# Mixture-of-experts layers in a two-block transformer kernel: quarter-width expert matmuls, neighbouring-row weight layout, and projection weights loaded one stage earlier

## The chip, the cores and the metric

The kernel runs on one core of one Trainium2 chip. The metric is the device time of one execution in microseconds (us). Three runs of the kernel before took 3566.93, 3572.45 and 3578.07 us; the median is 3572.45 us.

## The reference, cut to what matters

The program is two transformer blocks on 512 tokens of width 1024, all in float32. The first block has two layers; each ends in a mixture of experts, and these two mixtures are what the change rewrites. Per layer there are 16 experts, and each token goes to two of them:

```
def expert_block(args):
    xb, e = args
    hb = jax.nn.silu(xb @ w_gate[e]) * (xb @ w_up[e])
    return hb @ w_down[e]
...
x = layer_norm(ALPHA * x + moe(x, router_w, router_b, exp_w_gate[i], exp_w_up[i], exp_w_down[i]),
               ln_g[i, 1], ln_b[i, 1])
```

`w_gate[e]` and `w_up[e]` are 1024x512, `w_down[e]` is 512x1024, so one expert has three matrices of 2 MB. After the first layer's mixture comes an mLSTM mixer, whose input projection reads `ml_w_in`; after the second layer's mixture comes the second block, whose input projection reads `w_in_2` (the latent columns first). The second block ends in another expert stage of its own (16 experts of width 2048, called `ec` below), which the change leaves alone.

## The kernel before, in words

Each mixture is three stages, made by `moe_layer`. Between stages all engines meet at a barrier.

**route** (L1081). VectorE picks two experts per token and gives each token two rows in blocks of 96 rows, one expert to a block. SyncE meanwhile loads the three matrices of the first block. ScalarE has no work here.

**moe_experts** (L1247). The blocks are worked in pairs, r = 0 and r = 1, in a loop; in the profiled run a layer has 16 blocks in 8 pairs. Weights have two sets of buffers, one for each r. `moe_load` (L1242) brings one matrix with one DMA: row k*128+p of the matrix goes to partition p, so a partition gets 8 separate runs of 512 values (2 KB each) of gate and of up, and 4 runs of 1024 values (4 KB) of down. For one block TensorE does:

- `turn_x` (L1332): 8 transposes, in two halves of 4, bring the block's 96 rows of x into columns; ScalarE copies each half to `xg`. The second half uses the same PSUM bank as the first.
- `gate_up` (L1341): rows 0 to 63; 64 columns of the array do gate and the other 64 do up, 16 matmuls with 512 columns of the moving operand. A float32 matmul shows as two instructions, so 32 in the trace.
- `gate_up_tail` (L1352): rows 64 to 95; four strips of 32 columns of the array, each with a quarter of gate and up together, 32 matmuls (64 instructions) with 256 columns.
- ScalarE makes the sigmoid and copies the up half to SBUF, VectorE multiplies twice, for main and tail apart.
- `turn_h` (L1362): 6 matmuls with the identity bring the hidden rows into columns in the bank `h_ps`; VectorE copies them to `hT` (L1438, L1439).
- `down` (L1377): 64 rows in two halves of the array (16 instructions at L1385), then 32 rows in four strips (32 instructions at L1390). ScalarE empties the two banks (`rows_out`, L1481, L1482), GpSimd stores them to HBM (L1517, L1519).

The order on TensorE is written out by hand in `body`:

```
gate_up(i, 0)
turn_x(2 * i + 1, 1, i, 0)
gate_up_tail(i, 0)
turn_x(2 * i + 1, 1, i, 1)
gate_up(i, 1)
gate_up_tail(i, 1)
turn_h(i, 0)
...
```

and goes on with turn_x, down(i, 0), turn_x, turn_h(i, 1), down(i, 1). SyncE's queue (`load_pair`) reloads a buffer when it is free: gate and up of block r after its tail, down of both blocks after their `down`. The first block's x comes from 64 one-hot matmuls (`first_x`); GpSimd scatters all of x to HBM with 8 indirect DMAs, and later blocks' rows are read back from there (L1287).

**expert_sum** (L900). Two gathers per token tile, the weighted sum, the layer norm, and x transposed into `xT` for the next stage. SyncE is done after a few small loads.

Then `mlstm_inputs` (L1653) starts its own loads (L1694 to L1706): the gate columns `wg`, the first 384-column chunk, two copies of the gate bias, the convolution weights, the second chunk. Its first matmuls (L1739) wait for `wg` and both copies of the bias. In the second block, `gemms` (L157), called for "proj2", queues eight small side loads and then the first two weight chunks (L152); its first matmuls (L245) wait for chunk 0.

## Time and profile before

| what | value |
|---|---|
| median of three runs | 3572.45 us (3566.93 to 3578.07) |
| the profiled execution | 3572.37 us, its span 3570.0 us |
| TensorE (PE) busy | 3086.9 us, 86% |
| VectorE (DVE) busy | 1253.6 us, 35% |
| ScalarE (ACT) busy | 620.4 us, 17% |
| GpSimd (POOL) busy | 341.8 us, 10% |
| DMA | 886.20 MB, mean 248 GB/s |
| first block's mixtures | from 377 to 780 us and from 1150 to 1570 us of the span |
| the `ec` stage | about 2600 us to the end, 422 GB/s throughout |

A row of the timeline gives start, duration, engine, line, what is written from what, the count of instructions merged, and in brackets the idle time of the engine before it with what ended it. A matmul's duration is modelled and overlaps the next one's, so the distance between the starts of two groups is the time that the first one takes.

### The profile page before, as it was taken

The numbers are of one execution on the slowest core, as the hardware profiler recorded it, in microseconds if no ns is written. First come the engines' busy times: TensorE is split into PE (matmuls) and PEld (weight loads), VectorE is DVE, ScalarE is ACT, GpSimd is POOL, SyncE is SP. The second block draws the span as 40 slices with busy tenths as digits, with TensorE's granted clock in tenths as the row PEclk, the third lists the DMA queues.
The fourth block names the chain that finished last, engine by engine and source line by source line (L and its number), as shares of the span: only waits on it lengthen the run. The fifth ranks groups of instructions, "written<-read, shape, count | busy, mean of one in ns | idle before, by whom it ended". The sixth has DMA issues, their size and how long they took to land. (4 is left out here: it accounts for less than half of the span.)

```text
span 3570.0 us, 45399 instructions
## 1 busy us (share of the span) xinstructions
PE 3086.9 (86%) x17819; PEld 1460.8 (41%) x17819; DVE 1253.6 (35%) x2822; ACT 620.4 (17%) x1334; POOL 341.8 (10%) x434
## 2 busy tenths in 40 slices
PE   8889699949968799839999999889879888888887
PEld 5455444424444444324444444476433222332232
DVE  6533211133262111134999951175332111211122
ACT  1143122131321122130010021154100000000001
POOL 0023011110201111101000000014100000000000
PEclk9989799969988899959999999999889999999999
DMA  7861799922011999635333543591679999999997
GB/s 264 228 252 66 255 362 359 328 93 67 12 48 43 347 355 357 224 112 189 106 106 121 135 171 106 204 355 43 235 289 422 422 422 422 422 422 422 422 422 299
DMA packets 282432, 886.20 MB, mean 248 GB/s; under 512 B 35704, under 2 KB 75520, under 8 KB 233168
## 3 DMA queue, kind: packets, MB, share of 16 engines
q1 hardware_dynamic: 254032, 806.79, 60.3%
q0 software_dynamic: 28288, 77.91, 6.2%
q8 instruction: 71, 1.16, 0.1%
q14 instruction: 41, 0.34, 0.0%
HBM read 803.59 MB, written 80.99 MB: 248 GB/s over the span
## 5 line engine op out<-in xcount | busy, mean ns | idle before, releaser
L3060 PE MATMUL ec_gu<-ec_ring,ec_xg 128*32 128x512 f32 x4096 | 472.6, 605 | 98.3 <-DMA ec_ring<-in_w_up 97.4
L245 PE MATMUL proj_ps<-xT,proj_w 128*128 128x512 f32 x992 | 431.2, 597 | 0.0
L245 PE MATMUL proj_ps<-proj_w,xT 128*128 128x512 f32 (+2 forms) x896 | 360.7, 565 | 21.7 <-DMA proj_w<-in_w_in 21.7
L3060 PEld LDWEIGHTS ec_gu<-ec_ring,ec_xg 128*32 128x32 f32 x4096 | 123.6, 111 | 439.6 <-issue 295.3
L245 PEld LDWEIGHTS proj_ps<-xT,proj_w 128*128 128x128 f32 x992 | 189.5, 192 | 237.8 <-issue 237.6
L245 PEld LDWEIGHTS proj_ps<-proj_w,xT 128*128 128x128 f32 x896 | 172.4, 193 | 208.2 <-issue 156.3
L1349 PE MATMUL moe_gu_ps<-moe_w,moe_xg 128*64 128x512 f32 x1024 | 226.8, 595 | 18.4 <-ACT moe_xg L1464 16.8
L3096 PE MATMUL ec_yp<-ec_ring,ec_hT 128*64 128x512 f32 x1024 | 225.7, 595 | 7.0 <-issue 5.3
L274 ACT ACTIVATE proj_o<-proj_ps 128x512 f32<-128x512 f32 (+1 forms) x120 | 70.8, 590 | 611.4 <-PE proj_ps L245 611.3
L2239 DVE SCALAR_TENSOR_TENSOR band_big<-proj_hit,proj_row,band_big 128x516 f32<-128x516 f32 x256 | 173.5, 750 | 2.4
L2239 DVE SCALAR_TENSOR_TENSOR band_acc<-proj_hit,proj_row,band_acc 128x512 f32<-128x512 f32 x256 | 172.5, 746 | 2.4
L3153 DVE TENSOR_TENSOR xT<-xT,ec_gu 128x512 f32<-128x512 f32 x32 | 22.0, 688 | 374.6 <-ACT xT L3222 374.6
L1428 DVE TENSOR_TENSOR moe_sig<-moe_sig,moe_gu_ps 64x512 f32<-64x512 f32 x32 | 21.8, 680 | 374.2 <-ACT moe_up L1470 374.2
L3222 ACT ACTIVATE xT<-ec_gu 128x512 f32<-128x512 f32 x32 | 19.1, 598 | 771.1 <-PE ec_gu L3060 771.1
L1385 PE MATMUL moe_y_ps<-moe_w,moe_hT 128*64 128x512 f32 x512 | 125.4, 635 | 19.7 <-DVEq L1441 19.7
L3096 PEld LDWEIGHTS ec_yp<-ec_ring,ec_hT 128*64 128x64 f32 x1024 | 77.7, 137 | 142.8 <-issue 137.4
L1349 PEld LDWEIGHTS moe_gu_ps<-moe_w,moe_xg 128*64 128x64 f32 x1024 | 72.0, 137 | 154.0 <-issue 154.0
L1359 PE MATMUL moe_tgu_ps<-moe_w,moe_xg 128*32 128x256 f32 x2048 | 120.3, 388 | 0.0
L718 PE MATMUL mix_o<-out_w,xT 128*128 128x512 f32 x256 | 111.0, 593 | 2.6 <-PEq L89 2.6
L3183 DVE TENSOR_TENSOR ec_y<-ec_yp,ec_gate 64x512 f32<-64x512 f32 x32 | 22.0, 689 | 226.8 <-PE ec_yp L3096 226.6
L1748 PE MATMUL ml_ps<-xT,ml_w 128*128 128x512 f32 x224 | 96.4, 593 | 0.0
L1359 PEld LDWEIGHTS moe_tgu_ps<-moe_w,moe_xg 128*32 128x32 f32 x2048 | 64.2, 112 | 55.8 <-issue 16.9
(519 smaller groups left out, 3567.4 us busy)
## 6 DMA issues: line engine op xcount, KB each, us to landing
ec_ring<-in_w_gate SPq DMA_DIRECT2D x128, 1024.0 KB, 24.5
ec_ring<-in_w_up SPq DMA_DIRECT2D x128, 1024.0 KB, 27.0
ec_ring<-in_w_down SPq DMA_DIRECT2D x128, 1024.0 KB, 26.0
moe_w<-in_exp_w_gate SPq DMA_DIRECT2D x32, 2048.0 KB
moe_w<-in_exp_w_up SPq DMA_DIRECT2D x32, 2048.0 KB
moe_w<-in_exp_w_down SPq DMA_DIRECT2D x32, 2048.0 KB, 18.8
proj_w<-in_w_in SPq DMA_DIRECT2D x22, 2048.0 KB, 11.0
proj_w<-in_w_ada SPq DMA_DIRECT2D x16, 1536.0 KB
```

The costliest lines, as they stand in the source:

```text
L245: mm = nc.tensor.matmul(bank[0:jb["op"], 0:jb["ow"]], lhs, rhs, start=(k == 0), stop=(k == nk - 1))
L274: e = nc.scalar.activation(row, bank, jb["func"], scale=jb["scale"])
L718: mm = nc.tensor.matmul(o_ps[t % 2][q][:], xT[:, k, t * P:(t + 1) * P], w[q][:, k, :], start=(k == 0), stop=(k == KD - 1))
L1349: mm = nc.tensor.matmul(gu_ps[r][part, :], xg[r][:, k, 0:MAIN], w[r][n][:, k * D_EXP:(k + 1) * D_EXP], start=(k == 0), stop=(k == KD - 1))
L1359: mm = nc.tensor.matmul(tgu_ps[r][q * TAIL:(q + 1) * TAIL, :], xg[r][:, k, MAIN:MB], w[r][n][:, c0:c0 + 256], start=(k == 0), stop=(k == K ...
L1385: nc.tensor.matmul(y_ps[part, :], hT[r][:, f, 0:MAIN], w[r][2][:, c0:c0 + 512], start=(f == 0), stop=(f == KF - 1))
L1748: mm = nc.tensor.matmul(bank[:], w[m % 2][:, kk, g * P:(g + 1) * P], xT[:, kk, :], start=(kk == 0), stop=(kk == KD - 1))
L2239: V.scalar_tensor_tensor(acc[:, h, 0:wd], self.hit[r][:, 0:wd], self.row[r][:, h:h + 1], acc[:, h, 0:wd], ALU.mult, ALU.add)
L3060: mm = nc.tensor.matmul(gu_ps[2 * g + m][q * TG:(q + 1) * TG, :], xg[:, k, c0:c0 + TG], cols[:, :, q, :], start=(k == 0), stop=(k == KD - 1))
L3096: mm = nc.tensor.matmul(y_ps[half, :], hT[:, f * CAP:(f + 1) * CAP], w[:, j * D + hh * 512:j * D + (hh + 1) * 512], start=(f == 0), stop=( ...
L3153: V.tensor_mul(hid[g], sig[g], gu_ps[2 * g][:])
L3183: e = V.tensor_mul(y[lo if ex == 0 else hi, n_of(hh)], y_ps[half, :], gt2[half, n_of(hh)])
```

## The change

- The expert matrices are laid out with neighbouring rows in a partition: row 8p+k of gate and up, row 4p+k of down. A partition's share of a matrix is one run of 16 KB in HBM. Gate and up of one r lie in one buffer `gu`.
- x must match: in route, ScalarE copies each token tile of x (128x1024) into the space of `xT` so that columns p*8+k become k*128+p; `first_x` and the scatter read this copy.
- Gate and up of all 96 rows are computed as three groups of 32 rows in four strips of the array, 96 matmuls with 256 columns per block; the moving operand is 128 columns of gate and 128 of up. The hidden rows come out as 32-row strips, so VectorE's 32x32 transpose makes `hT` directly. `turn_h`, the ScalarE copies of up, `h_ps` and the two VectorE copies go.
- The order on TensorE becomes gate_up(0), gate_up(1), turn_x, down(0), turn_x, down(1); `turn_x` has two banks. The first pair is written out ahead of the loop with turn_x(1) between its gate_ups.
- ml_w_in's gate columns and first two chunks, and proj2's first two chunks, are loaded by SyncE during expert_sum, after its gathers have landed. Each set of buffers is freed later with one more barrier.

```
@@ expert_sum, SyncE
+                if ahead:
+                    for t in range(NT):
+                        sp.wait_ge(got[t], 32)
+                    ahead(sp)
@@ route
+            @block.scalar
+            def _(act):
+                xp = rows_by_partition(xT)
+                for t in range(NT):
+                    nc.scalar.activation(xp[:, t, :].rearrange("a (k p) -> a k p", p=P),
+                                         x[:, t, :].rearrange("a (p k) -> a k p", p=P), ACT.Copy)
@@ moe_load
-    sp.dma_start(w[n][:], weights[n][ds(e, 1)].rearrange("a (k p) n -> p (a k) n", p=P)).then_inc(w_ready[n], 16)
+    sp.dma_start(w[n], weights[n][ds(e, 1)].rearrange("a (p k) n -> p (a k) n", p=P)).then_inc(w_ready[n], 16)
@@ moe_experts
+        cols_of = lambda r, k, q: gu[r][:].rearrange("p (m k q c) -> p m k q c", m=2, k=KD, q=Q)[:, :, k, q, :]
@@ SyncE, load_pair
                     for r in range(2):
-                        sp.wait_ge(turned, 4 * i + 2 * r + 3)
+                        sp.wait_ge(turned, 4 * i + 2 * r + 2)
                         rows(2 * i + 2 + r, r)
-                        sp.wait_ge(tail_ready, 2 * i + r + 3)
+                    for r in range(2):
+                        sp.wait_ge(gu_ready, 4 * i + 2 * r + 2)
                         moe_load(sp, w[r], w_ready[r], weights, 0, e[r])
                         moe_load(sp, w[r], w_ready[r], weights, 1, e[r])
@@ TensorE
+                    pe.wait_ge(gu_taken, 2 * b + 1)
+                    for g in range(GROUPS):
+                        for k in range(KD):
+                            for q in range(Q):
+                                mm = nc.tensor.matmul(gu_ps[r][q * TAIL:(q + 1) * TAIL, g * 256:(g + 1) * 256],
+                                                      xg[r][:, k, g * TAIL:(g + 1) * TAIL], cols_of(r, k, q),
+                                                      start=(k == 0), stop=(k == KD - 1))
+                        if g >= 1:
+                            mm.then_inc(gu_ready, 1)
...
+                def downs(i, more):
+                    for r in range(2):
+                        if more:
+                            turn_x(2 * i + 2 + r, r, i + 1 + r)
+                        down(i, r)
                 def body(i, more):
                     gate_up(i, 0)
                     gate_up(i, 1)
+                    downs(i, more)
...
+                gate_up(0, 0)
+                turn_x(1, 1, 1)
+                gate_up(0, 1)
+                downs(0, True)
+                with pe.Fori(1, n1) as i:
                     body(i, True)
@@ VectorE, for the pieces (groups 0 and 1, group 2)
+                        V.tensor_mul(sig[r][:, g, :], sig[r][:, g, :], gu_of(r)[:, g, 0, :])
+                        V.drain()
+                        V.tensor_mul(hid[r][:, g, :], sig[r][:, g, :], gu_of(r)[:, g, 1, :]).then_inc(gu_taken, 1)
+                        V.drain()
+                        e = V.transpose(hT[r][:].rearrange("p f (g t) -> p g f t", t=TAIL)[:, g, :, :],
+                                        hid[r][:, g, :].rearrange("p g (t f) -> p g f t", t=TAIL))
@@ mlstm_inputs
-                pe.wait_ge(g_in, 48)
+                pe.wait_ge(wg_in, 16)
@@ class MixerWeights
+    def fetch(self, sp):
+        sp.dma_start(self.wg[:], self.cols[:, :, 2 * ML_W:2 * ML_W + 16]).then_inc(self.wg_in, 16)
+        self.load(sp, 0)
+        self.load(sp, 1)
@@ second_block
-                gemms(nc, "proj2", jobs, ahead=(begin[id(gate_job)] - 1, bb.first),
+                gemms(nc, "proj2", jobs, ahead=(begin[id(gate_job)] - 1, bb.first), held=ws[0], begun=2,
...
+            nc.clear_and_free_semaphores(ws[0].ready)
+            nc.all_engine_barrier()
```

In `mlstm_inputs` the gate bias now has a semaphore of its own, on which VectorE waits before it uses the bias. `wg`, the chunk buffers and their semaphores move to `MixerWeights`.

## Rows read from the trace of the kernel before

**Rows 1.** The page's costliest groups: gate and up of rows 0 to 63.

```profile
L1349 PE MATMUL moe_gu_ps<-moe_w,moe_xg 128*64 128x512 f32 x1024 | 226.8, 595 | 18.4 <-ACT moe_xg L1464 16.8
```

**Rows 2.** Busy time by stretches: two pairs; then PEclk, DMA share, GB/s.

```profile
534.09:573.46 39.37, 37.19 (x332) 16.71 (x328) 5.54 (x12) 8.88 (x17) 6.09 (x12) 1.00 1.04 357
653.91:694.99 41.08, 38.91 (x333) 17.12 (x329) 5.54 (x12) 8.88 (x17) 6.09 (x12) 0.96 1.04 357
```

**Rows 3.** Timeline of TensorE in the pair that starts at 534.09.

```profile
534.09 7.09 PE L1349 MATMUL moe_gu_ps<-moe_w,moe_xg 128*64 128x512 f32 x32
541.10 0.55 PE L1337 MATMUL moe_x_ps<-ident,moe_xs 96*128 96x96 f32 x4
541.58 3.66 PE L1359 MATMUL moe_tgu_ps<-moe_w,moe_xg 128*32 128x256 f32 x64
545.17 0.55 PE L1337 MATMUL moe_x_ps<-ident,moe_xs 96*128 96x96 f32 x4
...
559.79 3.65 PE L1385 MATMUL moe_y_ps<-moe_w,moe_hT 128*64 128x512 f32 x16 [0.43 <-DVEq L1441]
563.38 1.93 PE L1390 MATMUL moe_ty_ps<-moe_w,moe_hT 128*32 128x256 f32 x32
565.24 0.55 PE L1337 MATMUL moe_x_ps<-ident,moe_xs 96*128 96x96 f32 x4
```

**Rows 4.** DMA totals of two stretches: 534.1:573.5, and 2700:3400.

```profile
DMA packets 5842, 14.05 MB, mean 357 GB/s; under 512 B 325, under 2 KB 325, under 8 KB 5842
...
DMA packets 40555, 295.34 MB, mean 422 GB/s; under 512 B 4505, under 2 KB 4505, under 8 KB 4505
```

**Rows 5.** Timeline of that pair: GpSimd stores what ScalarE has emptied.

```profile
567.01 1.12 POOL L1517 DMA_DIRECT2D slots<-moe_y  x2 [27.38 <-ACTq L1483]
```

**Rows 6.** Timeline of TensorE: starts of pairs, last down of layer 0.

```profile
407.78 7.09 PE L1349 MATMUL moe_gu_ps<-moe_w,moe_xg 128*64 128x512 f32 x32 [0.88 <-ACT moe_xg L1464]
...
455.33 7.09 PE L1349 MATMUL moe_gu_ps<-moe_w,moe_xg 128*64 128x512 f32 x32
...
694.99 7.09 PE L1349 MATMUL moe_gu_ps<-moe_w,moe_xg 128*64 128x512 f32 x32
...
732.02 1.93 PE L1390 MATMUL moe_ty_ps<-moe_w,moe_hT 128*32 128x256 f32 x32
1181.60 7.09 PE L1349 MATMUL moe_gu_ps<-moe_w,moe_xg 128*64 128x512 f32 x32 [0.86 <-ACT moe_xg L1464]
...
1228.48 7.09 PE L1349 MATMUL moe_gu_ps<-moe_w,moe_xg 128*64 128x512 f32 x32
...
1469.84 7.09 PE L1349 MATMUL moe_gu_ps<-moe_w,moe_xg 128*64 128x512 f32 x32
```

**Rows 7.** Timeline of the first pair in layer 0, then layer 1.

```profile
420.46 0.90 PE L1337 MATMUL moe_x_ps<-ident,moe_xs 96*128 96x96 f32 x4 [5.60 <-DMA moe_xs<-slots]
421.29 5.82 PE L1359 MATMUL moe_tgu_ps<-moe_w,moe_xg 128*32 128x256 f32 x64
...
1190.86 0.38 SPq L1244 DMA_DIRECT2D moe_w<-in_exp_w_up  x1
...
1201.74 4.51 PE L1349 MATMUL moe_gu_ps<-moe_w,moe_xg 128*64 128x512 f32 x20 [1.60 <-DMA moe_w<-in_exp_w_up]
```

**Rows 8.** Timeline of route in layer 0: VectorE's last instruction.

```profile
395.36 0.15 DVE L1239 TENSOR_SCALAR blk_e<-route_nbl 128x1 int32<-128x1 f32 x1
```

**Rows 9.** Timeline: end of expert_sum, start of mlstm_inputs; proj2's start.

```profile
773.55 5.73 ACT L1049 ACTIVATE xT<-exp_t,exp_ccol 128x128 f32<-128x128 f32 x16
...
780.07 0.41 SPq L1694 DMA_DIRECT2D ml_wg<-in_ml_w_in  x1
...
788.14 8.41 PE L1739 MATMUL ml_ps<-xT,ml_wg 128*4 128x512 f32 x64 [12.43 <-DMA ml_gb<-in_ml_gate_bT]
...
1570.83 0.33 SPq L2148 DMA_DIRECT2D proj_pki<-in_pos_k  x1
...
1584.19 36.09 PE L245 MATMUL proj_ps<-proj_w,xT 128*128 128x352 f32 x112 [17.71 <-DMA proj_w<-in_w_in]
```

More of the change, by code:

```diff
@@ L897, in _, with expert_sum @@
                         e.then_inc(y_pool[i], 1)
-def expert_sum(nc, name, x, xT, ident, sbr, y, gain, shift, second=None, h=None):
+def expert_sum(nc, name, x, xT, ident, sbr, y, gain, shift, second=None, h=None, ahead=None):
     posA, posB, wA, wB, _ = sbr
@@ L1483, in rows_out, with rest @@
                     nc.scalar.drain().then_inc(y_copied, 1)
-                def body(i, more):
-                    main(i, 0)
-                    copy_x(2 * i + 1, 1, 0)
-                    tail(i, 0)
-                    copy_x(2 * i + 1, 1, 1)
-                    main(i, 1)
-                    tail(i, 1)
-                    if more:
-                        copy_x(2 * i + 2, 0, 0)
-                    rows_out(i, 0)
-                    if more:
-                        copy_x(2 * i + 2, 0, 1)
-                    rows_out(i, 1)
-                copy_x(0, 0, 0)
-                copy_x(0, 0, 1, h_ps)
-                with act.Fori(0, n1) as i:
+                def rest(i, more):
+                    for r in range(2):
+                        if more:
+                            copy_x(2 * i + 2 + r, r)
+                        rows_out(i, r)
+                def body(i, more):
+                    gates(i, 0)
+                    gates(i, 1)
+                    rest(i, more)
+                copy_x(0, 0)
+                gates(0, 0)
+                copy_x(1, 1)
+                gates(0, 1)
+                rest(0, True)
+                with act.Fori(1, n1) as i:
                     body(i, True)
@@ L3249, in second_block, with latent_weights, fetch @@
     with nc.sbuf_tensor("h", [P, NT, D], F32) as h, ExitStack() as held:
+        n_lat = Q_RANK + KV_RANK + ROPE
+        hf = h[:].rearrange("p t d -> p (t d)")
+        rows = hf[:, 0:NT * n_lat].rearrange("p (t f) -> p t f", t=NT)
+        lat_job = job(win, 0, 2, n_lat // 2, xT, P, S, None, "N",
+                      sb=lambda j, g: rows[:, g, j * (n_lat // 2):(j + 1) * (n_lat // 2)])
+        first = ExitStack()
+        ws = []
+        def latent_weights():
+            ws.append(WeightSlots(nc, first, "proj2", 2, KD * 512, False, side="right"))
+            def fetch(sp):
+                for j in range(2):
+                    ws[0].load(sp, lat_job, j, j)
+            return fetch
         moe_layer(nc, 1, a, x, xT, cst, slots, y_dram, sbr, escore,
-                  [ln(a["ln_g"][1, 1], a["ln_b"][1, 1]), rms(a["g_norm_mix_2"][0], sh1, sc1)], h=h)
-        n_lat = Q_RANK + KV_RANK + ROPE
+                  [ln(a["ln_g"][1, 1], a["ln_b"][1, 1]), rms(a["g_norm_mix_2"][0], sh1, sc1)], h=h, ahead=latent_weights)
         gates = dram("gates", [S, 2 * D])
```

221 lines of the change are left out of this document (85 added, 136 removed).

## The prediction

> **What bounds the kernel now.** I first read the page's table of busy shares: TensorE is busy 86% of the span, so a change pays where it shortens TensorE's own sequence or a wait in it. The page's costliest groups then say who is waited for in the mixtures: the idle time ahead of gate and up was ended by ScalarE's copy of x, 16.8 of 18.4 us, and not by the weight loads [rows 1]. So the mixture loop runs at TensorE's pace.
>
> The busy times by stretches show how near the next limit is. In one pair of blocks, 39.37 us, TensorE is busy 37.19 us, and the DMA engines have a share of 1.04 at 357 GB/s [rows 2]: they are full too. The DMA totals say with what: 5842 packets for 14.05 MB, every one under 8 KB. From 2700 to 3400 us, in the `ec` stage, 36,050 of 40,555 packets are 8 KB or more and the same engines move 422 GB/s [rows 4]. Two things hold the pair near 39.4 us, and a change of one alone gives little.
>
> The timeline of TensorE prices the parts of a pair by the distance between starts [rows 3]: 64 instructions of the tail 545.17 - 541.58 = 3.59 us, half a turn of x 541.58 - 541.10 = 0.48 us, the two parts of down 3.59 and 1.86 us, together 5.45 us. A second kind of pair takes 41.08 us instead of 39.37, at a mean granted clock of 0.96 instead of 1.00 [rows 2]: in it a short stretch runs at 1.2 GHz, for 1.7 us more. Three of the layer's pairs 1 to 6 in layer 1 and two in layer 0 are of that kind.
>
> **The change, part by part.**
>
> *A steady pair.* Gate and up of a block become 192 instructions of the tail's form, 128 rows by 32 columns of the array with 256 moving columns: 3 x 3.59 = 10.77 us, 21.54 us for two. Column work is what it was (the old parts take 7.01 + 3.59 = 10.60 us), only the moving operand lies in two runs. No row here has two runs in just this way; the cost of that is between nothing (the `ec` stage feeds four runs of 128 columns) and a few per cent, and I take nothing. Four half turns are 1.92 us, two downs 10.90 us. Sum 34.36 us. `turn_h` and the waits for VectorE's copies of it go, and so does ScalarE's copy of x between two gate_ups, since a block's x is now turned a whole down ahead. VectorE gets a 32x32 transpose instead, beside TensorE's other work: gate_up(1) and a turn cover block 0's chain, turn and down(0) cover block 1's.
>
> What is late next: down(1) waits until ScalarE has emptied the banks of down(0), and only one turn of x, 0.96 us, is left in between where turn_h stood. GpSimd, which waits for the same signal, starts at 567.01, 1.77 us after down(0) ends at 565.24 [rows 3, 5]. The bounds are 0 and 1.77 - 0.96 = 0.8 us; GpSimd's own start is in that, so I take 0.5 us. A steady pair: 34.9 us.
>
> *Can DMA keep up?* A pair needs 12.58 MB of weights and 1.57 MB of x and y rows. One run of 16 KB per partition makes a packet at least as long as the `ec` stage's. At 422 GB/s the weights take 29.8 us; the small rows at today's 357 take 4.4 us; 34.2 us, just under 34.9. Buffers give room besides: gate and up of block 0 are issued at 10.8 us of a pair and needed at 34.9, and take 10 us. So TensorE still sets the pace. The upper bound is today's 357 GB/s, 39.6 us a pair (a rival below). DMA is the next bound, at once.
>
> *Pairs 1 to 6.* Layer 0: 694.99 - 455.33 = 239.7 us now, 6 x 34.9 = 209.4 after, 30.3 less. Layer 1: 1469.84 - 1228.48 = 241.4, 32.0 less [rows 6]. That counts the slow-clock stretches as gone, since TensorE's gaps shrink to one of 0.5 us a pair; if they stay in every pair it is 12 x 1.7 = 20 us worse.
>
> *The last pair.* Now 694.99 to 732.02 + 1.93, 39.0 us. After: 21.54 + 5.45 + 5.45 us and, with no turn between the downs, a wait of about 1.5 us: 33.9. 5.1 us less in each layer, 10.2 us.
>
> *The first pair* takes 47.55 us in layer 0 and 46.88 in layer 1 [rows 6]. gate_up(0, 0) is 10.8 us. The x rows of block 1 come only after the scatter, at 420.46, 12.7 us after the pair's start, so TensorE waits about 2 us instead of 5.6 [rows 7]. Then gate_up(0, 1) stands ahead of what used to fill the time, and waits for up of block 1. In layer 1 that load is issued 9.3 us into the pair (1190.86 - 1181.60) and ended a wait 10.9 us later, at 20.1 [rows 6, 7]. With longer packets it lands between 5.0 us after the x rows (2.1 MB at 422), at 17.7, and those 20.1; I take 18.7, nearer the first, since the stage with long packets is the nearest row for them. Behind such a wait the clock is at 1.2 GHz for a while: the tail at 421.29 took 5.8 us where 3.6 is usual [rows 3, 7], 2.2 us more. 18.7 + 10.8 + 2.2 + 13.3 (turns, downs, 0.5 wait) = 45.0 us. 2.5 and 1.9 us less.
>
> *Route.* ScalarE gets four copies of 128x1024 with a stride of 8 elements in the read. By its row with 16 pieces of 128 columns in 5.73 us [rows 9], 1024 columns take at most 2.9 us if the stride is free, four 11.5 us, and the stride may add to that. They stand beside VectorE's chain, which ends at 395.36, 18 us after the stage begins [rows 8]. I take nothing; without that cover it would be the 11.5 us and more. The gathers' and scatters' sizes don't change.
>
> *Early loads.* In mlstm_inputs the first matmul started at 788.14, 8.1 us after the stage's first instruction, held by the last small load [rows 9]. After, `wg` and chunk 0 have landed; VectorE still waits for the bias, but needs it only when the gate matmuls (8.4 us) are done. TensorE starts at about 780.4: 7.7 us less. In proj2 the first matmul goes from 1584.19 to about 1571.1: 13.1 us less. VectorE and ScalarE work there on what TensorE delivers, so they move with it and I count the gain as kept. The loads themselves, 3 MB at most, run in expert_sum behind its gathers, where no other large transfer is. SyncE waits there for the gathers, and nothing is queued behind it. Two added barriers: from ScalarE's last end, 773.55 + 5.73 = 779.28, to the next stage's first instruction, 780.07, is 0.8 us [rows 9]; 1.6 us more.
>
> *Sum:* 30.3 + 32.0 + 10.2 + 2.5 + 1.9 + 7.7 + 13.1 - 1.6 = 96.1 us less. Against the profiled execution's 3572.4 us that is 3476.3. The median shown, 3572.45, is the same to 0.1 us. About 0.3% (11 us) is what a measurement of this kernel can tell from no change.
>
> **The rivals.**
>
> *Slow clock stays or comes.* Every steady pair has a stretch at 1.2 GHz, 1.7 us each. For it: the rows have it in five of twelve pairs, always in the later down. Against: the gaps ahead of it shrink. 3476 + 20 = 3496. Chance 0.10.
>
> *The early loads buy nothing*, because another engine or load sets those stages. Against: TensorE waits for exactly these transfers [rows 9]. 3476 + 21 = 3497. Chance 0.06.
>
> *DMA becomes the bound* at today's 357 GB/s, because the loads' rate is not set by the packets, or because they stay cut at 2 KB. Then a pair takes 14.15 MB / 357 = 39.6 us. The buffers' room, some 7 us at the first steady pair, is eaten at 4.7 us a pair, so some 4.5 of six pairs pay 4.7 us: 21 us a layer, 42 in all, 3518. Against it: 422 GB/s with 8 KB packets on the same engines [rows 4], and there each load of 1 MB to 128 partitions already travels as runs of 8 KB. The Trainium skill's page "DMA: Bandwidth & Descriptors" (Specifications) speaks for this rival: it says that transfers of 512 B and up reach line rate, and gives about 358 GB/s as a core's share of HBM, so 16 KB runs would bring nothing over 2 KB. By that rule the time would be 3518. The trace has exactly such a figure, 357, in the mixtures, but the 422 of the `ec` stage goes against both halves of it. Chance 0.11.
>
> *Slower than before.* A single run of 16 KB into one partition might be worse than short ones: only 8 such packets an engine per matrix, and the stores of y take turns with them. It decides where DMA time per pair passes today's 40 us by more than the rest gains, at some 14.15 MB / 42 us = 337 GB/s. At 300 GB/s a pair takes 47.2 us, 7 us more than now in 12 pairs, 84 us, less about 20 us of early loads: 3572 + 64 = 3636. No row has packets over 8 KB in numbers; up to 8 KB longer was faster. Chance 0.04. A change that comes to nothing by several of these together has 0.02.
>
> **How the numbers follow.** The forecast has a chance of 0.67, so the predicted time is its 3476. Its own range comes from the bounds: 7 us less without the wait for emptied banks, 4 us less in the first pairs, 2 to 3 us in the early loads, so 3462; and 5 to 10 us more from two runs in the moving operand and half the slow stretches. With the first two rivals the range reaches to 3508, which leaves out DMA's two cases and the last, 0.17. Faster by over 0.3%: 0.94; within: 0.02; slower: 0.04.
>
> **What would show it.** Right: distances of 34.5 to 35.5 us between starts of pairs; DMA packets of 16 KB, some 128 per matrix, and over 400 GB/s while loads run; a DMA share clearly under 1.0 at times; idle time ahead of down(1) ended by ScalarE; first matmuls of mlstm_inputs and proj2 within 1 us of their stages' starts. Wrong: idle time ahead of gate_up ended by a weight load in steady pairs; gate_up over 11.2 us a block; ScalarE's four copies ending after VectorE's chain in route; the first pair over 48 us.

## The result, and the profile after

The changed kernel takes 3472.87 us (median of 4 runs), the kernel before 3574.84 on the same chip: ratio 0.971, 95% interval 0.9693 to 0.9728, 102 us less. The prediction was 3476.3. That the number fits hides two errors of 15 and 13 us that cancelled, and a third in what was credited to the early loads. The profiled execution of the changed kernel is the fastest of its four (3464.36 us; the others 3466.67, 3479.07 and 3480.73), so the profiles show a larger difference than the medians. First the page of the changed kernel: span, TensorE, the group that answers to [rows 1], all packets of the execution.

```profile
span 3462.0 us, 50697 instructions
PE 3025.1 (87%) x20507; PEld 1482.5 (43%) x20507; DVE 1244.6 (36%) x2822; ACT 576.8 (17%) x1266; POOL 341.6 (10%) x434
...
DMA packets 212814, 886.41 MB, mean 256 GB/s; under 512 B 35704, under 2 KB 75520, under 8 KB 151248
...
L1366 PE MATMUL moe_gu_ps<-moe_gu,moe_xg 128*32 128x256 f32 x6144 | 338.4, 382 | 8.7 <-DMA moe_gu<-in_exp_w_up 7.5
```

TensorE is busy 2% less. ScalarE's copy of x no longer ends the idle time ahead of gate and up. The packets went from 282432 to 212814, 69618 fewer: 64 gate and up matrices less 896 packets each and 32 down matrices less 384 each would be 69632, so the long runs are there.

A layer has eight pairs, counted 0 to 7: pair 0 is the first, pairs 1 to 6 are the steady ones, pair 7 is the last. The timeline of TensorE, an undisturbed pair (it answers to [rows 3]), and a later one:

```profile
483.90 20.90 PE L1366 MATMUL moe_gu_ps<-moe_gu,moe_xg 128*32 128x256 f32 x384
504.73 0.88 PE L1353 MATMUL moe_x_ps<-ident,moe_xs 96*128 96x96 f32 x8
505.55 3.65 PE L1380 MATMUL moe_y_ps<-moe_w,moe_hT 128*64 128x512 f32 x16
509.13 1.93 PE L1385 MATMUL moe_ty_ps<-moe_w,moe_hT 128*32 128x256 f32 x32
510.99 0.88 PE L1353 MATMUL moe_x_ps<-ident,moe_xs 96*128 96x96 f32 x8
512.23 3.65 PE L1380 MATMUL moe_y_ps<-moe_w,moe_hT 128*64 128x512 f32 x16 [0.36 <-ACTq L1460]
515.81 1.93 PE L1385 MATMUL moe_ty_ps<-moe_w,moe_hT 128*32 128x256 f32 x32
517.56 20.90 PE L1366 MATMUL moe_gu_ps<-moe_gu,moe_xg 128*32 128x256 f32 x384
...
608.63 0.88 PE L1353 MATMUL moe_x_ps<-ident,moe_xs 96*128 96x96 f32 x8 [2.08 <-DMA moe_xs<-slots]
609.44 5.35 PE L1380 MATMUL moe_y_ps<-moe_w,moe_hT 128*64 128x512 f32 x16
```

The undisturbed pair is 517.56 - 483.90 = 33.66 us. The later one waits 2.08 us for the x rows of the next pair, and behind that wait the same 16 instructions take 5.35 us instead of 3.65. Six pairs of the twelve steady ones have such waits: 0.70, 2.08 and 0.57 us in layer 0, 0.17, 1.71 and 2.84 in layer 1, and the three of 1.7 us and more are each followed by a slow down. Pairs 1 to 6 average 34.5 us in layer 0 and 35.0 in layer 1.

Both kinds of pair by stretches (clock, DMA share and GB/s at the end, as in [rows 2]), then the DMA view of 455:645, its rate in 40 slices and its totals:

```profile
483.90:517.56 33.66, 33.30 (x500) 18.07 (x496) 5.02 (x12) 4.82 (x12) 6.09 (x12) 1.00 1.01 406
...
585.65:623.15 37.50, 35.07 (x500) 18.48 (x496) 5.00 (x12) 4.81 (x12) 6.09 (x12) 0.95 1.01 401
```

```profile
GB/s 422 326 396 425 428 435 420 425 371 357 401 438 406 432 438 422 327 365 424 428 434 421 424 372 311 414 435 428 428 428 415 287 381 428 428 415 437 424 350 336
DMA packets 8507, 76.39 MB, mean 402 GB/s; under 512 B 1807, under 2 KB 1807, under 8 KB 4401
```

The engines are as full as before by their share, but move 402 GB/s instead of 357 [rows 2]. The rate is not even: about once a pair it falls to some 290 to 370. That dip turned out to be the story behind the waits: two blocks need 12.58 MB of weights and 1.57 MB of rows, and 14.15 MB at 402 GB/s take 35.2 us, more than the 33.66 us of TensorE. The undisturbed pair above moves 406 GB/s x 33.66 us = 13.67 MB, so the transfers fall behind by 0.5 MB in it; the buffers hide that for some pairs, then TensorE waits.

Where the 108.0 us of the two profiled executions went (spans 3570.0 and 3462.0), by distances between marks in the two timelines: expert stage of layer 0 from first gate and up to last down 326.2 to 284.3 (41.9 less), layer 1 327.2 to 286.6 (40.7), from the experts' end to the mixer's first matmul 54.2 to 45.9 (8.3), to the last projection's 75.4 to 61.4 (14.0), mixer to the next experts 393.5 to 388.3 (5.2), ahead of the first experts 1.6 less, behind the last projection's start 3.6 more. The forecast's 96.1 us had 76.9 in the experts (82.6 here) and 19.2 in the early loads with their barriers (22.3 here); the other 3.2 it did not have.

### The profile page after: what moved, and what is told of

It is laid out like the page before. It is cut to its first block and busy times, and to the rows that moved or that the text cites. A ratio compares the mean times of both kernels' runs of the same rounds, so it can differ in the third digit from the quotient of the medians.

```text
span 3462.0 us, 50697 instructions
## 1 busy us (share of the span) xinstructions
PE 3025.1 (87%) x20507; PEld 1482.5 (43%) x20507; DVE 1244.6 (36%) x2822; ACT 576.8 (17%) x1266; POOL 341.6 (10%) x434
## 2 busy tenths in 40 slices
DMA packets 212814, 886.41 MB, mean 256 GB/s; under 512 B 35704, under 2 KB 75520, under 8 KB 151248
## 5 line engine op out<-in xcount | busy, mean ns | idle before, releaser
L1366 PE MATMUL moe_gu_ps<-moe_gu,moe_xg 128*32 128x256 f32 x6144 | 338.4, 382 | 8.7 <-DMA moe_gu<-in_exp_w_up 7.5
L1366 PEld LDWEIGHTS moe_gu_ps<-moe_gu,moe_xg 128*32 128x32 f32 x6144 | 201.4, 111 | 142.0 <-issue 11.1
L1421 DVE TENSOR_TENSOR moe_sig<-moe_sig,moe_gu_ps 128x256 f32<-128x256 f32 x64 | 22.7, 355 | 482.8 <-ACT moe_sig L1452 482.8
L1752 PE MATMUL ml_ps<-xT,mlw 128*128 128x512 f32 x224 | 96.4, 593 | 0.0
L3035 PE MATMUL ec_x<-ec_sel,h 128*128 128x128 f32 x576 | 70.9, 283 | 11.1 <-ACT ec_xg L3219 6.2
L3035 PEld LDWEIGHTS ec_x<-ec_sel,h 128*128 128x128 f32 x576 | 67.5, 196 | 19.7 <-ACT ec_xg L3219 7.9
## 6 DMA issues: line engine op xcount, KB each, us to landing
moe_w<-in_exp_w_down SPq DMA_DIRECT2D x32, 2048.0 KB, 18.7
```

Of the source, the lines that this page charges most:

```text
L1366: mm = nc.tensor.matmul(gu_ps[r][q * TAIL:(q + 1) * TAIL, g * 256:(g + 1) * 256], xg[r][:, k, g * TAIL:(g + 1) * TAIL], cols_of(r, k, q), ...
L1752: mm = nc.tensor.matmul(bank[:], w[m % 2][:, kk, g * P:(g + 1) * P], xT[:, kk, :], start=(kk == 0), stop=(kk == KD - 1))
L3035: mm = nc.tensor.matmul(x_ps[:, c * P:(c + 1) * P], h[:, t, cc * P:(cc + 1) * P], sel[:, t, :], start=(t == 0), stop=(t == NT - 1))
```

## The experiments

Twelve kernels, numbered by subject, not in the order in which they ran. Times are medians, ratios are against runs of the kernel before on the same chip. The experiments ran on several chips, on which the kernel before has medians from 3572.66 to 3578.16 us, and each median stands for 4 to 10 runs: a difference of some 5 us between two of the kernels below is not told from none by their medians, and the traces have to tell it. The length of a pair is the distance between the starts of its gate and up and the next one's.

**1. Short runs again for gate and up.**

```
-                                         x[:, t, :].rearrange("a (p k) -> a k p", p=P), ACT.Copy)
+                                         x[:, t, :].rearrange("a (k p) -> a k p", p=P), ACT.Copy)
...
-    sp.dma_start(w[n], weights[n][ds(e, 1)].rearrange("a (p k) n -> p (a k) n", p=P)).then_inc(w_ready[n], 16)
+    rows = "a (k p) n -> p a k n" if n < 2 else "a (p k) n -> p a k n"
+    src = weights[n][ds(e, 1)].rearrange(rows.replace("p a k n", "p (a k) n"), p=P)
+    sp.dma_start(w[n], src).then_inc(w_ready[n], 16)
```

> The changed kernel with its gate and up matrices loaded as before the change (128 partitions times 8 runs of 2 KB per matrix, instead of 16 KB in one run), and x copied by ScalarE without the reordering; the down matrices keep the long runs, the narrow matmuls and the early loads stay. Theory A (the long runs are what lets the queue keep up with the faster loop): the two gate and up pairs of matrices, 8.39 MB, go at the old 357 GB/s, 23.5 us, the other 5.3 MB at the new 405, 13.0 us, so a pair takes about 36.5 us or more where the changed kernel's undisturbed pairs take 33.66 and its mean of pairs 1 to 6 is 34.5 and 35.0; the DMA's share stays at 1.00 and the rate falls from 402 towards 375 GB/s. Time 3473 + 12 x 1.5 to 12 x 2.9 = 3491 to 3508. Theory B (the length of a run doesn't matter here, TensorE alone sets the pair): pairs stay at 33.7 to 35, time 3473 within 5 us.

Measured: 3509.54 us, ratio 0.9816 (0.98 to 0.9832), 36.7 more than the changed kernel. Timeline of TensorE in pair 2 of layer 0, and the DMA view of 455:645:

```profile
508.54 1.52 PE L1355 MATMUL moe_x_ps<-ident,moe_xs 96*128 96x96 f32 x8 [2.54 <-DMA moe_xs<-slots]
509.99 4.64 PE L1382 MATMUL moe_y_ps<-moe_w,moe_hT 128*64 128x512 f32 x16
```

```profile
GB/s 423 428 250 310 388 388 397 405 428 436 236 322 387 387 402 406 428 432 234 335 387 386 402 406 444 411 234 348 387 389 398 414 432 407 225 365 386 391 398 420
DMA packets 25743, 71.50 MB, mean 376 GB/s; under 512 B 1628, under 2 KB 1628, under 8 KB 24436
```

Theory A holds: from pair 2 on every pair waits, 37.4 to 38.3 us in layer 0 and 37.8 to 40.7 in layer 1, at 376 GB/s. It came out 1.5 us above the upper end (3508). The expectation had divided 13.67 MB, what an undisturbed pair moves; a pair needs 14.15 MB, and at 376 GB/s these take 37.6 us, as in layer 0. Layer 1's pairs of 40.4 us are longer than that; in nine of the ten pairs that wait the first 16 matmuls of a down take 4.6 to 6.1 us instead of 3.65, and whether that is what lengthens them was not tested. The narrow matmuls need the long runs.

**2. Long runs alone, in the kernel before.** The load of gate and up takes `(p k)`, ScalarE's four copies are added in `route`, the experts read `rows_by_partition(xT)`; nothing else.

> The kernel before with one part of the change alone: gate and up matrices in 16 KB runs and x reordered by ScalarE into xT during the routing stage, which the expert stage reads as its rows; half-width matmuls, short runs of the down matrices and late loads stay. Theory A (the old loop was set by TensorE, 39.37 us a pair with its queue at the limit beside it): the pairs stay at 39.0 to 39.4, time 3570 to 3575. Theory B (the old loop was set by the queue): pairs fall to about 36.5 as two thirds of its bytes go faster, 14 x 2.5 = 35 us less, 3535 to 3545.

Measured: 3575.64 us, ratio 0.9999 (0.9989 to 1.0008). Two pair starts (the first gate and up of a pair has no wait):

```profile
495.97 7.09 PE L1362 MATMUL moe_gu_ps<-moe_w,moe_xg 128*64 128x512 f32 x32
508.61 7.09 PE L1362 MATMUL moe_gu_ps<-moe_w,moe_xg 128*64 128x512 f32 x32 [1.00 <-ACT moe_xg L1477]
535.35 7.09 PE L1362 MATMUL moe_gu_ps<-moe_w,moe_xg 128*64 128x512 f32 x32
```

39.38 us a pair, as before. So the long runs of gate and up alone are worth nothing: the old loop was set by TensorE. The pairs of 41.0 to 41.1 us are still there too, one in layer 0 and four in layer 1.

**3. Late loads.** Both early loads undone: `mw.fetch(sp)` is the first thing of the mixer's input stage, and the last projection has `begun=0`.

> The changed kernel with both early loads undone: the first weights of the mLSTM input stage are asked for when that stage begins, as before, and none of the weights of the last projection is asked for ahead of its stage; the expert stages are those of the change. Theory A (each stage began with a wait for its weights that the early load removes): first matmul of the mLSTM inputs 8 us later against the end of the experts (45.9 us there in the changed kernel, 54.2 in the one before), that of the last projection 14 us later (61.4 against 75.4): 3473 + 22 = 3495. Theory B (the loads only take up the queue earlier and what they gain is lost again in the summing stage): within 5 us of 3473.

Measured: 3492.10 us, ratio 0.9777 (0.9754 to 0.98), 19.2 more than the changed kernel, near theory A's 22. The profiled execution is the fastest of its four (3475.88; the others 3491 to 3505), so the marks in the trace carry more than the median. They divide it otherwise. Timeline of TensorE, first matmul of each of the two stages, here and in the changed kernel:

```profile
737.28 9.79 PE L1744 MATMUL ml_ps<-xT,mlw_g 128*4 128x512 f32 x64 [6.59 <-DMA mlw_g<-in_ml_w_in]
...
1485.99 34.37 PE L245 MATMUL proj_ps<-proj_w,xT 128*128 128x352 f32 x108 [17.88 <-DMA proj_w<-in_w_in]
```

```profile
736.39 8.72 PE L1743 MATMUL ml_ps<-xT,mlw_g 128*4 128x512 f32 x64 [4.40 <-PEq L89]
...
1472.62 40.31 PE L245 MATMUL proj_ps<-proj_w,xT 128*128 128x352 f32 x128 [4.40 <-PEq L89]
```

Against the experts' end the projection starts 13.6 us later (75.0 against 61.4), as expected. The mixer starts 2.4 us later (48.3 against 45.9) and not 8. The rest must come from something that this experiment left in: the gate bias.

**4. x rows ahead of the down matrices.**

```
 def load_pair(i):
-    for r in range(2):
-        sp.wait_ge(turned, 4 * i + 2 * r + 2)
-        rows(2 * i + 2 + r, r)
...
     for r in range(2):
+        sp.wait_ge(turned, 4 * i + 2 * r + 6)
+        rows(2 * i + 4 + r, r)
         sp.wait_ge(down_ready, 2 * i + r + 1)
         moe_load(sp, w[r], w_ready[r], weights, 2, e[r])
```

(With the first pair's rows asked for ahead of the loop, room for one more pair of rows, and TensorE's wait for them at the end.)

> The changed kernel with the rows of x of pair i+2 asked for as soon as those of pair i+1 have been transposed, so ahead of the down matrices in the queue instead of behind them (and one pair of rows too many at the end, that nobody reads). Theory A (the waits for x rows come of the order of the queue): the waits of 0.7, 2.1, 0.6 us in the first layer and 0.2, 1.7, 2.8 in the second go, 8.1 us, and with the three of 1.7 us or more the slow downs behind them (3 x 1.7 us): pairs 1 to 6 all at 33.7, time 3473 - 10 to 13 = 3460 to 3463. Theory B (the queue is full in this loop, share 1.01, so that something must be late): the same time is lost to waits for a gate, up or down matrix instead, the pairs still average 34.5 and 35.0, time 3470 to 3475.

Measured: 3477.20 us, ratio 0.9737 (0.972 to 0.9754). Waits of TensorE in layer 0 (us in total, times, longest), here and in the changed kernel:

```profile
PE moe_gu_ps L1368 <- DMA moe_gu<-in_exp_w_up: 20.2, 10, 4.1
PE moe_y_ps L1382 <- ACTq L1464: 3.7, 8, 1.2
```

```profile
PE moe_x_ps L1353 <- DMA moe_xs<-slots: 6.4, 4, 3.1
PE moe_y_ps L1380 <- ACTq L1460: 3.7, 8, 1.2
PE moe_gu_ps L1366 <- DMA moe_gu<-in_exp_w_up: 3.3, 1, 3.3
```

Theory B in its mechanism: no wait for x rows is left in the steady pairs, and nine more for a gate or up matrix took their place (ten against one); five of layer 0's six steady pairs take 34.4 to 38.2 us. It had 3470 to 3475 and the averages of before; layer 0 averages 36.6 us instead of 34.5, layer 1 34.4 instead of 35.0, and the median is 2.2 us above its range. Order in the queue was not what was short.

**5. Up of block 1 ahead of the wait for the scatter.** The second `moe_load` of block 1 moves above `sp.wait_ge(put, ...)`.

> The changed kernel with the up matrix of block 1 asked for before the queue waits for the scattered rows, not after it. Theory A (TensorE waits in the first pair for that matrix because SP sat in the wait): the 3.3 us and 4.2 us before gate and up of block 1 go, the first pair takes 40 instead of 44.0 and 43.3, time 3473 - 6 to 8 = 3465 to 3467. Theory B (the queue is full, the rows of block 1 are then later by the 5 us that 2 MB take): the wait moves to the transposition of block 1, which waits 3.1 and 3.0 us already, and the first pair stays within 1 us of 44.0 and 43.3: no change.

Measured: 3469.04 us, ratio 0.9711 (0.9693 to 0.9729). The first pair of layer 0 in the timeline, here and in the changed kernel:

```profile
423.57 1.54 PE L1353 MATMUL moe_x_ps<-ident,moe_xs 96*128 96x96 f32 x8 [5.90 <-DMA moe_xs<-slots]
425.69 12.61 PE L1366 MATMUL moe_gu_ps<-moe_gu,moe_xg 128*32 128x256 f32 x192 [0.58 <-ACT moe_xg L1445]
```

```profile
406.23 10.57 PE L1366 MATMUL moe_gu_ps<-moe_gu,moe_xg 128*32 128x256 f32 x192 [0.58 <-ACT moe_xg L1445]
419.89 1.54 PE L1353 MATMUL moe_x_ps<-ident,moe_xs 96*128 96x96 f32 x8 [3.09 <-DMA moe_xs<-slots]
424.74 12.74 PE L1366 MATMUL moe_gu_ps<-moe_gu,moe_xg 128*32 128x256 f32 x192 [3.31 <-DMA moe_gu<-in_exp_w_up]
```

Theory B: the wait for the matrix went (0.58 us is left), that for the rows grew from 3.09 to 5.90, and the first pairs are 43.96 and 43.15 us, where they were 44.01 and 43.28. In this trace layer 0's steady pairs have no wait at all (all 33.66 or 33.67 us) and three of layer 1's wait 0.92 to 3.14 us, with the edit outside the steady pairs: how many of them wait differs from one execution to the next.

**6. Both edits together.**

> Rows ahead and up first in one kernel. Theory A: the sum of the two, 3473 - 16 to 20 = 3453 to 3457. Theory B (the queue is full in the pairs, so moving loads in it can't shorten them): 3470 to 3475.

Measured: 3479.42 us, ratio 0.9739 (0.9714 to 0.9764). No gain, as theory B said, but 4.4 us above its range; in the trace layer 0's pairs 1 to 6 take 218.2 us and layer 1's 203.5, where the changed kernel has 207.2 and 210.2, and the waits are for gate and up matrices.

**7. Less traffic: no y stores in the loop.** GpSimd's `store` keeps its wait and its release of the buffer and loses the six transfers.

> The changed kernel without the y stores inside the loop (GpSimd only hands the buffers back; the last pair's stores stay), so the sums behind it read other rows: a part of the traffic is left out, nothing else. Theory A (the loop's transfers fill the 16 engines, and the waits for x rows are what does not fit): 0.79 of 13.67 MB a pair goes, the queue needs 12.88 / 0.406 = 31.7 us, the DMA's share falls to about 0.94, all pairs 1 to 6 take 33.66 and the slow downs behind the waits go: 3473 - 13 = 3460, and the first pair is shorter by up to 1 us. Theory B (the waits come of the place of the x rows in the queue, behind the down matrices, with room in the queue): waits of 0.6 to 2.8 us stay, 3473 within 5.

Measured: 3456.94 us, ratio 0.9679 (0.9658 to 0.9701), 15.9 less than the changed kernel. All twelve steady pairs take 33.66 to 33.71 us: theory A for the time. Not for the share. The DMA view of one pair, 484:517.6, slices of 0.84 us:

```profile
GB/s 488 390 390 488 429 449 410 390 488 361 327 244 224 361 176 244 283 307 380 468 390 390 488 371 429 468 429 449 410 390 488 371 410 468 449 449 390 410 488 371
DMA packets 1082, 13.27 MB, mean 395 GB/s; under 512 B 128, under 2 KB 128, under 8 KB 320
...
q1 hardware_dynamic: 1082, 13.27, 101.1%
```

SP's queue alone fills the engines, at a lower rate, where it had 94.5% beside the stores. So a share of 1.0 doesn't say that no more bytes would fit: there are nine slices in a row, 7.6 us, in which the engines are busy and move 176 to 361 GB/s. The record of single packets says the same: from 492 to 499.5 us a packet of 16 KB takes 0.89 us on average, where it takes 0.62 before and after. No store is in this kernel, so the dip isn't theirs. The two 384 KB loads of x rows, issued at 484.0, land 15.5 us later in the median, at about 499.5, as the dip ends. The dip is not gone here, and still no steady pair waits: the 13.37 MB that are left to a pair take 34.2 us at the 391 GB/s of 455:645, and the buffers cover six times 0.5 us.

**8. Short runs in all three matrices.** Experiment 1 with each down matrix in four transfers of 4 KB runs.

> The kernel of the first experiment (gate and up in 2 KB runs, 3509.5 us) with the down matrices too in four transfers of 4 KB runs each instead of one of 16 KB, so that every matrix has the runs of before and only the narrow matmuls, the layout in SBUF and the early loads are left of the change. Theory A (every byte then goes at the 357 GB/s of the old loop): 13.67 MB / 357 = 38.3 us a pair as the least, against the 37.5 and 39.5 that the first experiment's pairs average: pairs 38.3 to 41, time 3510 to 3530. Theory B (4 KB is long enough, 2 KB alone is short): the same as the first experiment within 5 us, 3505 to 3514.

Measured: 3513.99 us, ratio 0.9826 (0.9809 to 0.9843), 4.5 us over experiment 1, whose interval (0.98 to 0.9832) it overlaps. 364 GB/s in 455:645, against 376. Inside both theories' ranges, so not settled: 4 KB runs of the down matrices cost 4.5 us or nothing. It shows what the narrow matmuls are worth without any long run: the expert stages take 313.0 and 303.2 us here, against 326.2 and 327.2 in the kernel before and 284.3 and 286.6 in the changed one, so 37 of the 83 us gained there. Its pairs 1 to 6 average 39.2 us in layer 0, where 14.15 MB at 364 GB/s would take 38.9.

**9. 128 rows of x in a load instead of 96.**

```
-        xs = [st.sb(f"xs{r}", [MB, D]) for r in range(2)]
+        xs = [st.sb(f"xs{r}", [P, D]) for r in range(2)]
...
-                    sp.dma_start(xs[r][:], slots_dram[ds(b * MB, MB), :]).then_inc(xs_ready[r], 16)
+                    sp.dma_start(xs[r][:], slots_dram[ds(b * MB, P), :]).then_inc(xs_ready[r], 16)
```

(The transposes read `xs[r][0:MB, ...]`.)

> The changed kernel with 128 rows of x in each load of a block instead of 96 (the 32 more are the next block's and are not used): 0.26 MB more a pair. Theory A (96 rows use 96 of the 128 partitions and so only part of the paths into SBUF, which is why the rate falls to 176 to 361 GB/s while they land): the dip goes, 1.05 MB at 406 take 2.6 us where 0.79 MB at 270 take 2.9, pairs the same or shorter, 3465 to 3473. Theory B (the reads of the rows themselves are slow, whatever they are written to): 1.05 MB at 270 take 3.9 us, 1.0 more a pair, the waits for x rows grow by that in pairs 2 to 6 of each layer and bring more slow downs: 3480 to 3490.

Measured: 3451.00 us, ratio 0.9649 (0.9628 to 0.9671), 21.9 less than the changed kernel, and the fastest of all. The DMA view of 455:645 and a pair's row among the busy times by stretches:

```profile
GB/s 423 414 439 415 439 421 417 434 417 436 422 428 438 422 430 423 426 432 421 431 417 436 438 406 436 424 428 425 432 437 401 443 425 431 428 422 433 404 445 431
DMA packets 9150, 81.07 MB, mean 427 GB/s; under 512 B 1850, under 2 KB 1850, under 8 KB 4858
```

```profile
483.90:517.56 33.66, 33.30 (x500) 18.07 (x496) 5.01 (x12) 4.82 (x12) 6.08 (x13) 1.00 1.01 427
```

Theory A. More bytes go and the dip is gone: no slice is under 401 GB/s. All twelve steady pairs take 33.66 or 33.67 us and no down runs slow. The two profiled executions differ by 11.7 us (3450.3 and 3462.0), 3.5 of it in layer 0's experts and 8.3 in layer 1's; the medians differ by more. The changed kernel's four runs spread over 16 us and these over 7, and experiment 5 shows its waits differing between executions; that this makes up the rest is likely and not shown. The packets tell the same as the rate: from 495 to 503 us, while the 128 rows of two blocks land, one of 16 KB takes 0.61 us and one of the rows 0.16, where 96 rows took 0.26 each in experiment 7.

The Trainium skill bears on this: its page "SBUF — State Buffer" (Door 1: The DMA port swizzle) says that a transfer's bandwidth depends on how many of 16 ports its partitions reach, with partitions 0 to 63 on eight of them and 64 to 127 on the other eight. Rows 0 to 95 then load eight ports twice as much as the rest. This agrees in direction. By that rule alone 96 rows take as long as 128, so padding would cost nothing but gain nothing either; the measured gain is larger than that, and which engine writes which row no run here shows.

**10. x rows through GpSimd's queue.** GpSimd asks for block b + 4 right before it stores block b.

> The changed kernel with the x rows of blocks 1 and later asked for by GpSimd in its own queue, right after the down matmuls that free the buffer's y, instead of by SP behind the down matrices. Theory A (in the loop the 16 engines have only just enough time, whatever the queue, as the fourth and the seventh experiment say): x rows never wait, but a gate or up matrix does, as in the fourth experiment: pairs 1 to 6 average 34.5 to 36, time 3470 to 3480. Theory B (what costs the time is that the x rows go in one lump through one queue: in the DMA view of the seventh experiment's pair the rate is 390 to 488 GB/s except for 6.7 us at 176 to 361 in the stretch where they land; beside the weights of the other queue they are spread out): no wait for rows nor for matrices, pairs 1 to 6 all at 33.7, 3473 - 13 = 3460, and no slice of a pair under 350 GB/s.

Measured: 3501.29 us, ratio 0.9795 (0.9775 to 0.9814), 28.4 more than the changed kernel; neither theory had that. Timelines of GpSimd and of TensorE in layer 0:

```profile
472.48 0.52 POOL L1482 DMA_DIRECT2D moe_xs<-slots  x1 [16.43 <-issue]
473.12 1.13 POOL L1501 DMA_DIRECT2D slots<-moe_y  x2
```

```profile
523.48 1.54 PE L1349 MATMUL moe_x_ps<-ident,moe_xs 96*128 96x96 f32 x8 [5.99 <-DMA moe_xs<-slots]
```

The first pairs wait 10.6 and 9.8 us for rows (49.1 and 47.6 us instead of 44.0 and 43.3), every second pair after them 2.7 to 6.5 us, and slices of 275 to 331 GB/s remain in the DMA view of 480:530. GpSimd waits for its stores to land before it goes on, and 384 KB of rows now stand in the same queue ahead of them; that this is what delays it is my reading. As a test of spreading the rows it is spoilt by that, and settles nothing.

**11. The bias's wait alone, in the kernel before.** `pe.wait_ge(g_in, 48)` becomes 16, and the two bias loads count on a semaphore that VectorE waits for.

> The kernel before with one wait moved: in the mLSTM input stage TensorE waits for its gate weights alone, and the gate bias has a semaphore of its own that VectorE waits for, as in the changed kernel; all loads stay where they were. Theory A (the start at 788.14 was held by the bias, a transfer of 0.1 KB that stands behind 1.5 MB of the first weight chunk in the queue, and the early load itself is worth only the 2.4 us that the third experiment showed): first matmul 2.2 us after the first issue at about 780.1, so near 782.5, 5.7 us earlier, the chunk behind it then waits for its own 1.5 MB until some 786 or not at all as the gate matmuls take 8.4 us; time 3575 - 5 = 3570. Theory B (the weights set the start): 788.1 as before, no change.

Measured: 3573.92 us, ratio 0.9994 (0.9985 to 1.0004): as a time not to be told from no change, nor from the 4.6 us below, as the interval goes from 5 us less to 1 us more. The profiled execution is the second slowest of ten (3581.74 us): all its twelve steady pairs take 41.07 us, where the kernel before has five such in its profile, on the same code. The timeline shows the start:

```profile
790.15 8.68 PE L1740 MATMUL ml_ps<-xT,ml_wg 128*4 128x512 f32 x64 [7.85 <-DMA ml_wg<-in_ml_w_in]
```

The idle time ahead of that matmul is 12.43 us in the kernel before [rows 9], 7.85 here, 6.59 with late loads, 4.40 in the changed kernel. So 4.6 us of the 8.0 belong to the bias, which no longer holds TensorE from behind the first 1.5 MB of weights, and 2.2 to the early load; 1.3 lie in other differences between this kernel and that of experiment 3.

**12. Short runs of gate and up with 128 rows.**

> The first experiment's kernel (gate and up in 2 KB runs, 3509.5 us, 36.7 more than the changed kernel) with 128 rows of x in each load of a block, as in the ninth, which took the changed kernel to 3451 us with all its pairs at 33.66 and a rate of 427 GB/s without a dip. Theory A (2 KB runs are slower in themselves: in the DMA view of the first experiment the gate and up matrices go at 382 to 410 GB/s outside the dip): 8.39 MB / 390 = 21.5 us and the other 5.96 MB at 427 = 14.0, 35.5 us a pair as the least against 33.66 that TensorE needs; 3451 + 12 x 1.8 = 3473 at least, with slow downs 3473 to 3490. Theory B (the dips of the 96 rows were all that made the short runs matter): pairs at 33.7, 3451 to 3458.

Measured: 3477.88 us, ratio 0.9725 (0.9708 to 0.9741). From pair 4 on, 35.65 to 35.70 us in both layers, against theory A's 35.5; TensorE's wait in such a pair:

```profile
601.27 3.01 PE L1368 MATMUL moe_gu_ps<-moe_gu,moe_xg 128*32 128x256 f32 x52 [1.34 <-DMA moe_gu<-in_exp_w_up]
```

Theory A: 404 GB/s in 455:645 against 427, and 14.42 MB at 404 GB/s take 35.7 us, which is what the pairs take. Single packets show why: outside any dip one of 2 KB takes 84 to 88 ns, one of 4 KB 159, one of 8 KB 313 (`ec` stage of the kernel before, 2700 to 3400 us), one of 16 KB 612, so 23 to 24 bytes per ns for the shortest and 26.8 for the longest. So the 36.7 us of experiment 1 are not the price of short runs alone: with 128 rows they cost 26.9 us (3477.88 - 3451.00), and what is late is a gate or up matrix instead of the rows.

## Why the prediction was right, and where it was not

*A steady pair*: predicted 34.9 us, measured 33.66. The two gate_ups take 504.73 - 483.90 = 20.83 us, 54.2 ns an instruction, where 56.1 came from the old tail's 64 instructions; that row held the start of a phase in every 64, and six phases in a row have fewer seams, which is my reading, not a test. Turns 0.82 and 0.88 us instead of 1.92 together; downs 5.44 and 5.33 where 5.45 was taken; the wait for emptied banks 0.36 us where 0.5 was taken, 1.16 in the last pair where 1.5 was.

*Can DMA keep up?* This is the step that failed. It said 34.2 us of transfers in 34.9 us, so "TensorE still sets the pace", with the weights at 422 GB/s and the rows at 357, 414 together. The 14.15 MB were right, but the rate is 402, so 35.2 us: while 96 rows land, everything on the engines falls to 176 to 361 GB/s (experiment 7). That is more than the 33.66 us of TensorE and more than the forecast's 34.9; the buffers cover it for some pairs, and six of twelve wait, 8.1 us and 5.0 us of slow downs, 13 in all. By luck twelve pairs at 1.24 us under the forecast are worth 15. Experiment 9 shows the cause: without the dip the engines move 427 GB/s, which is what 14.42 MB in 33.66 us ask for, and no steady pair waits. Behind the wrong rate stands a wrong reading of [rows 4]. I took all of the difference between 357 and 422 GB/s for the price of short packets. But a loop that TensorE paces moves 14.15 MB in 39.37 us whatever the engines could do, which is 359 GB/s, so the 357 was no measure of their limit (the new loop with the same runs, which does wait for its transfers, gets 364, experiment 8); and the kernel before has the dip as well, as its rate in 455:645 shows:

```profile
GB/s 409 412 343 293 387 311 313 392 408 412 401 248 377 361 257 379 405 410 415 286 331 389 269 340 397 409 415 308 304 374 295 317 370 381 394 420 269 338 381 257
```

With 2 KB runs of gate and up the new loop moves 376 GB/s with the dip and 404 without (experiments 1 and 12), with 16 KB runs 402 and 427: the dip costs 25 to 28 GB/s, the short runs of gate and up 23 to 26. My sign for room, a DMA share clearly under 1.0, never came, not even with fewer bytes; it is no measure of room.

*Pairs 1 to 6* together: 207.2 and 210.2 us, predicted 209.4, by the luck above. *Last pair*: 33.0, predicted 33.9. *First pair*: 44.0 and 43.3, predicted 45.0; gate_up(0, 1) starts 18.5 and 18.7 us into it, predicted 18.7. That the late issue of up of block 1 makes that wait is right only in part: asked for earlier (experiment 5), the matrix swaps places with the rows and the pair stays as long.

*"A change of one alone gives little"*: right for the long runs of gate and up (experiment 2: nothing, within 0.1%), wrong for the narrow matmuls, which alone bring 37 us in the experts (experiment 8). I had the queue at 357 GB/s full and took that for no room, but short runs give 364 to 376 there, and the buffers let the first pairs run at 33.7 us. On top of the narrow matmuls the long runs are worth 36.7 us, and 26.9 with 128 rows.

*Route*: ScalarE's four copies take 7.84 us from 374.63, and VectorE's chain ends at 393.07. Hidden, as predicted.

*Early loads*: proj2 13.1 predicted, 13.6 shown by experiment 3. The mixer's 7.7 was right as a distance and wrong as a cause: I had read [rows 9]'s "held by the last small load" and still booked all of it on the early load. That load is worth 2.4 us (2.2 by the idle time in experiment 11); 4.6 belong to the bias's own semaphore, which the diff also made. 4.40 us of idle time, ended by the barriers, are left ahead of both stages.

*Not predicted*: 5.2 us between the mixer's start and the next experts. The scan's code is unchanged, yet the kernel before waits there once for VectorE:

```profile
963.04 2.30 PE L1947 MATMUL scan_n<-mli_v,scan_wt 128*128 128x193 f32 x6 [2.25 <-DVE scan_wt L2007]
```

and has a clock of 0.89 in the 30 us from 170 us into the mixer, where the changed kernel has no such wait and a clock of 1.00. The late-load kernel has the gain too (389.3 us), the bias kernel has not (394.8), so neither edit makes it. It is not chance between executions either: the stretch takes 393.5 to 394.8 us in the three traces with the old expert loop (kernel before, experiments 2 and 11), with a wait of 2.0 to 2.3 us there, and 388.3 to 392.8 in the eleven with the new one, with 1.0 us at most. What carries it from one stage to the next is open.

*The rivals*: "DMA becomes the bound" was half true: full engines and waits in half the pairs, but at 402 GB/s, not at 357. With its condition met, every matrix in short runs, the time is 3514 (experiment 8), where it said 3518. The rule of the Trainium skill cited there (page "DMA: Bandwidth & Descriptors", Specifications), line rate from 512 B up and about 358 GB/s as a core's share, does not hold here, where one core runs alone: experiments 9 and 12 are equal but for the runs of gate and up and move 427 GB/s with 16 KB, 404 with 2 KB. "Slow clock stays" was right in three of twelve pairs, each behind a wait of 1.7 us or more. Its count from one profile was weak ground: the old loop, with gaps of 0.74 and 1.00 us in every pair, has the slow down in five of twelve pairs in one profile and in twelve of twelve in another (experiment 11).

## What to carry to other kernels

Where two engines are both near their limit, price the change as a pair: here 37 us for the one half, nothing for the other, 83 for both in the experts. To know whether transfers keep up, divide the bytes of a round by a rate taken where the work waits for its transfers: a loop that another engine paces moves what it is asked for, and its rate is no limit. When a loop's waits move from one load to another as you reorder the queue, stop reordering and look at the rate over time within one round: a dip with busy engines points to a transfer of a bad shape, and the cure may be to load more (128 partitions for 96). And when a stage starts late, read which transfer released it before crediting the load that you moved.

## What was not expected of the hardware

While loads of 96 partitions (384 KB each) land, the rate of the 16 engines together falls to between 176 and 361 GB/s (experiment 7), and the packets of other transfers slow down too: those of 16 KB in the same queue take 0.89 us instead of 0.62, the 2 KB stores of GpSimd's queue 121 ns instead of 84 (changed kernel, 495 to 502 us). The same load with 128 partitions runs at the full 427 (experiment 9); by what path the shape does this no run shows. The share of busy DMA engines stayed at 1.01 at 391, 402 and 427 GB/s alike. Runs of 2 KB make a pair 2.0 us longer even with no dip (35.7 against 33.66). In the steady pairs of the changed kernel waits of TensorE of 1.7 us and more were each followed by 16 matmuls in 5.3 instead of 3.65 us, waits of 0.7 us and less were not. The length of the wait alone does not decide it, though: in the kernel before the same 16 matmuls take 5.35 us in some pairs and 3.65 in others behind the same gap of 0.74 us, and in experiment 4 one of 1.95 us ahead of gate and up was followed by 12.25 us for the 192 instructions, and ones of 1.69 to 2.08 us by the usual 10.57.
